# The second mixers' attention loop: steps of four jobs in place of steps of one, and keys stored without zero halves

## The reference

```python
def hybrid_mixer(h, ...):                       # h: 256 x 1024
    (sb_q, sb_k, sb_v, nq, nkc, nvc, nks, nvs, nkw, nvw, ngate,
     dq, dk, dv, iq, ik, iw) = jnp.split(h @ w_in, offs, axis=-1)
    o_a = stick_breaking_attention(...)         # 4 heads
    o_b = nsa_attention(...)                    # 8 heads of 64, 2 groups of keys
    o_c = dsa_attention(...)                    # 4 heads of 64, one shared key head
    g_a, g_b, g_c = jnp.split(jax.nn.sigmoid(h @ w_gate), 3, axis=-1)
    merged = g_a * (o_a @ w_br_a) + g_b * (o_b @ w_br_b) + g_c * (o_c @ w_br_c)
    return merged @ w_out

# nsa_attention, per query block of 128:
#   g0 * (softmax over 15 compressed keys) + g1 * (softmax over selected keys)
#     + g2 * (softmax over the last 512 keys)      with 256 positions all blocks are selected
# dsa_attention, per query block: softmax over the 64 keys that the indexer scores highest
```

## Time and profile before

| | us |
|---|---|
| device time, median of 3 runs | 2225.49 |
| lowest and highest of the 3 | 2224.66, 2225.7 |
| the profiled execution's own time | 2224.94 |
| its span in the profile | 2223.1 |
| TensorE busy in the span | 2214.6 (100%) |
| VectorE busy | 1831.6 (82%) |
| ScalarE busy | 1129.0 (51%) |

### The profile page before, as it was taken

How to read it: one execution, slowest core, us unless ns; L and a number is a source line. 1 busy time by engine, 2 the same in 40 slices (tenths; PEclk the granted TensorE clock), 3 DMA queues, 4 the chain that set the end, 5 groups by cost and what they waited for, 6 DMA issues and landing times.

```text
span 2223.1 us, 42390 instructions
## 1 busy us (share of the span) xinstructions
PE 2214.6 (100%) x16116; PEld 2043.3 (92%) x16116; DVE 1831.6 (82%) x3007; ACT 1129.0 (51%) x1503; POOL 4.8 (0%) x10
## 2 busy tenths in 40 slices
PE   9999999999999999999999999999999999999999
PEld 8998999999998999999999889999999998999998
DVE  8888578888888668887988878888898887898887
ACT  5445565445444565444434676654454346766443
POOL 0000000000000000000000000000000000000000
PEclk9999999999999999999999999999999999999999
DMA  7555445555555445654556443555556545344663
GB/s 253 194 196 202 149 174 196 198 198 170 200 198 203 175 142 188 211 196 163 200 188 211 171 145 130 181 199 190 187 177 207 189 170 191 129 150 165 217 198 132
DMA packets 76816, 407.62 MB, mean 183 GB/s; under 512 B 9264, under 2 KB 9920, under 8 KB 44336
## 3 DMA queue, kind: packets, MB, share of 16 engines
q1 hardware_dynamic: 75792, 404.93, 53.0%
q10 hardware_dynamic: 720, 0.89, 0.1%
q0 software_dynamic: 208, 0.49, 0.1%
HBM read 405.23 MB, written 1.05 MB: 183 GB/s over the span
## 4 chain that ended last, share of the span: by engine, by line
PE 96%; DVE 3%; issue 1%; ACT 0%; DMA 0%; DVEq 0%; SPq 0%
PE ps_proj L684 13%; PE ps_aux L693 13%; PE ps_y L263 10%; PE ps_y L264 10%; PE ps_y L265 10%; PE ps_proj L688 7%; PE ps_aux L696 7%; PE ps_proj L1126 3%; PE ps_proj L1119 3%; PE ps_proj L1120 3%; PE ps_proj L263 2%; PE ps_proj L264 1%; PE ps_proj L265 1%; PE ps_aux L651 1%; PE ps_proj L651 1%; PE ps_aux L1963 1%
## 5 line engine op out<-in xcount | busy, mean ns | idle before, releaser
L130 DVE TENSOR_TENSOR w_lo_front<-w_raw_front,w_hi_front 128x2048 fp32r<-128x2048 f32 x238 | 544.0, 2286 | 36.4 <-ACT w_hi_front L105 36.2
L105 ACT CAST w_hi_front<-w_raw_front 128x2048 fp32r<-128x2048 f32 x238 | 453.0, 1903 | 179.4 <-PE ps_aux L696 144.8
L263 PE MATMUL ps_y<-hidden_lo,w_hi_back 128*128 128x256 f32 x1344 | 372.4, 277 | 0.1
L264 PE MATMUL ps_y<-hidden_hi,w_lo_back 128*128 128x256 f32 x1344 | 371.1, 276 | 0.0
L265 PE MATMUL ps_y<-hidden_hi,w_hi_back 128*128 128x256 f32 x1344 | 371.1, 276 | 0.0
L105 ACT CAST w_hi_back<-w_raw_back 128x1024 fp32r<-128x1024 f32 x248 | 259.9, 1048 | 145.8 <-PE ps_y L265 119.5
L887 ACT ACTIVATE silu_gate<-silu_gate 128x256 f32<-128x256 f32 x176 | 73.7, 418 | 508.7 <-DVE silu_gate L924 508.6
L684 PE MATMUL ps_proj<-xt_lo_hi,w_hi_front 128*128 128x512 f32 x1280 | 319.7, 392 | 0.0
L693 PE MATMUL ps_aux<-xt_lo_hi,w_hi_front 128*128 128x512 f32 x1280 | 319.6, 392 | 0.0
L130 DVE TENSOR_TENSOR w_lo_back<-w_raw_back,w_hi_back 128x1024 fp32r<-128x1024 f32 x248 | 302.3, 1219 | 6.0 <-ACT w_hi_back L105 5.1
L684 PEld LDWEIGHTS ps_proj<-xt_lo_hi,w_hi_front 128*128 128x128 f32 x1280 | 228.5, 188 | 39.5
(11 more groups left out here) (460 smaller groups left out, 3808.0 us busy)
## 6 DMA issues: line engine op xcount, KB each, us to landing
w_raw_front<-in_stream SPq DMA_DIRECT2D x251, 1024.0 KB, 4.9
w_raw_back<-in_stream SPq DMA_DIRECT2D x252, 512.0 KB, 3.5
m_rel_bias<-in_rel_bias SPq DMA_DIRECT2D x2, 2048.0 KB, 7.9
m_params<-in_params SPq DMA_DIRECT2D x2, 656.0 KB, 4.2
w_raw_front<-in_stream SPq DMA_DIRECT2D x4, 256.0 KB, 6.8
w_raw_front<-in_stream SPq DMA_DIRECT2D x2, 512.0 KB, 8.6
x<-in_x ACTq DMA_DIRECT2D x3, 256.0 KB, 6.8
out<-x SPq DMA_DIRECT2D x3, 256.0 KB, 2.3
```

The source lines that it names most:

```text
L105: self.nc.scalar.copy(self.hi[part][:, parity], self.raw[part][:, parity]).then_inc(self.hi_done[part], by)
L130: eng.tensor_tensor(self.lo[part][:, parity], self.raw[part][:, parity], self.hi[part][:, parity].bitcast(F32), ALU.subtract).then_inc(sel ...
L263: nc.tensor.matmul(out, ah, bl, start=start, stop=False)
L264: nc.tensor.matmul(out, al, bh, start=False, stop=False)
```

## The change

Five steps of four jobs (`QUADS`) take the place of twenty steps of one. In a step TensorE does the scores of all four jobs, then the values of the step before, then four gates with the transposes between them: two jobs' behind the first gate, one behind the second and one behind the third. The first job's transposes go to the lower half of `ps_y2` and the second's to the upper half, so that these two don't wait for each other. Score banks, maxima, sums and probabilities have four places in place of two or three. The outputs of a step are 256 columns, rounded in one pair of VectorE instructions in place of two pairs of 128. The weights' remainders and the sorting rounds stand at listed places in the step (`EARLY_LOW`, `MIDDLE_LOWS`, `LATE_LOWS`, `SORTS`). The keys are stored as `m2_kT`, 64 rows for each head of the pair, without the place for the other half (`m2_k_block`), and so without the clearing of it on GpSimd. After the loop the first two channel blocks of the branch products are done for the first six of their eight inputs before the last two of either.

```diff
-DSA_JOBS = [(p, i, 3) for p in range(DSA_HEADS // 2) for i in range(TT)]
+DSA_JOBS = [(p, i, 3) for i in range(TT) for p in range(DSA_HEADS // 2)]
 JOBS = NSA_JOBS + DSA_JOBS
...
+QUADS = len(JOBS) // 4
+LOOP_GATE = GATES - len(JOBS)
+def score_bank(s, job, e):
+    r, width = job % 4, (JOBS[job][1] + 1) * P
+    pair = (s.py[3], s.pa[1]) if r < 2 else (s.py[0], s.py[1])
+    return pair[e][:, r % 2 * width:(r % 2 + 1) * width]
+def quad_out(s, job):
     p, i, br = JOBS[job]
...
+    return s.pa[p if br == 3 else 0][:, i * P:(i + 1) * P]
...
+EARLY_LOW = {2: ((0, 13),)}
+MIDDLE_LOWS = {0: ((1, 10),), 1: ((1, 11), (0, 12)), 2: ((1, 13),), 3: ((1, 14), (0, 15)),
+               4: ((1, 15),)}
+LATE_LOWS = {0: ((0, 11),), 1: ((1, 12),), 2: ((0, 14),), 3: ((0, 16),),
+             4: ((1, 16), (0, 17), (1, 17))}
+SORTS = (3, 4, 5, 4)
...
-    m.pT = s.over_h
+    few = sb("m2_probsT_few", [P, 2, 2, P], F32)
+    m.pT = [few[:, 0], few[:, 1], s.over_h[:, 0], s.over_h[:, 1]]
     m.qT = sb("m2_qT", [P, 6, T], F32)
-    m.kbd = sb("m2_k_block", [P, NKV, 2, T], F32)
+    m.kT = sb("m2_kT", [P, NKV, T], F32)
...
-    m.scs = (sc[:, 0], sc[:, 1], zv[:, 0])
+    m.scs = (sc[:, 0], sc[:, 1], zv[:, 0], zv[:, 1])
...
     def turn(job):
-        i = JOBS[job][1]
+        r, i = job % 4, JOBS[job][1]
         need("probs_ready", job + 1)
-        if job >= 1:
+        if r != 1 and job > 0:
             need("probsT_ready", job)
+        bank = s.py[2][:, (r == 1) * 2 * P:]
         for e in range(2):
             for kc in range(i + 1):
                 j = e * (i + 1) + kc
-                last = nc.tensor.transpose(s.py[2][:, j * P:(j + 1) * P],
-                                           m.scs[job % 3][:, j * P:(j + 1) * P], s.ident[:])
+                last = nc.tensor.transpose(bank[:, j * P:(j + 1) * P],
+                                           m.scs[r][:, j * P:(j + 1) * P], s.ident[:])
         mark.inc(last, "probsT_done")
...
-    def values(job0):
...
+    def values(quad):
+        jobs = range(4 * quad, 4 * quad + 4)
+        if quad == 0:
             need("cs_ready", 1)
             need("pcT_ready", 1)
         else:
-            need("o_ready", pair)
-        for job in (job0, job0 + 1):
+            need("o_ready", quad)
+        need("probsT_ready", 4 * quad + 4)
+        for job in jobs:
             p, i, br = JOBS[job]
-            out = out_bank(s, job0)[:, (job % 2 if br == 3 else 0) * P:][:, 0:P]
             if br == 1:
-                nc.tensor.matmul(out, m.vbd[:, 2 * p:2 * p + 2].rearrange("p h d -> p (h d)"),
-                                 m.pcT[:, i * P:(i + 1) * P], start=True, stop=False)
-            need("probsT_ready", job + 1)
+                nc.tensor.matmul(quad_out(s, job), m.vbd[:, 2 * p:2 * p + 2].rearrange("p h d -> p (h d)"),
+                                 m.pcT[:, i * P:(i + 1) * P], start=i == 0, stop=False)
+        for job in jobs:
+            p, i, br = JOBS[job]
             for e in range(2):
                 for kc in range(i + 1):
                     v = {1: m.zi[:, kc, ZI_NVS + p // 2 * DH:][:, 0:DH],
                          2: m.zn[:, kc, ZN_NVW + p // 2 * DH:][:, 0:DH],
                          3: m.zn[:, kc, ZN_DV:ZN_DV + DH]}[br]
-                    last = nc.tensor.matmul(out[e * DH:(e + 1) * DH], v,
-                                            m.pT[:, job % 2, e * (i + 1) + kc],
-                                            start=br == 3 and kc == 0, stop=kc == i and br != 1)
-            mark.inc(last, "pv_done")
...
+    def scores(quad):
+        if quad >= 1:
+            need("biased", 4 * quad)
+        for job in range(4 * quad, 4 * quad + 4):
+            p, i, br = JOBS[job]
+            kv = {1: p // 2, 2: NSA_GROUPS + p // 2, 3: NKV - 1}[br]
+            qc = p + (NSA_HEADS // 2 if br == 3 else 0)
+            for e in range(2):
+                rows = slice(e * DH, (e + 1) * DH)
+                last = nc.tensor.matmul(score_bank(s, job, e), m.qT[rows, qc, i * P:(i + 1) * P],
+                                        m.kT[rows, kv, 0:(i + 1) * P])
+            mark.inc(last, "scores_done")
+    def branch(c, ks):
         q = P2_Y + c
-        if c < 2:
-            need("gate_ready", GATES - 1 + c)
-        else:
-            need("gated", 2 * (c - 1))
         hi, lo = w.chunk(pe, base, slot0 + q // 3, q % 3)
-        for k in range(8):
+        for k in ks:
             if c == 0 and k >= 2:
-                need("o_ready", {6: 11, 7: 12}.get(k, 2 * (k - 1)))
+                need("o_ready", k - 1)
             out = (s.pj[c % 2][:, 0:T] if k < 2 else s.pj[c % 2][:, T:2 * T] if k < 6
                    else s.pa[c % 2][:, 0:T])
             cols = slice(k * P, (k + 1) * P)
             last = product(nc, out, (hi[:, cols], lo[:, cols]), (m.oh[:, k], m.ol[:, k]),
                            k in (0, 2, 6), k in (1, 5, 7))
-        w.taken(last, q % 3)
+        if ks[-1] == 7:
+            w.taken(last, q % 3)
+    for quad in range(QUADS):
+        scores(quad)
+        if quad >= 1:
+            values(quad - 1)
+        gate(LOOP_GATE + 4 * quad)
+        turn(4 * quad)
+        turn(4 * quad + 1)
+        gate(LOOP_GATE + 4 * quad + 1)
+        turn(4 * quad + 2)
+        gate(LOOP_GATE + 4 * quad + 2)
+        turn(4 * quad + 3)
+        gate(LOOP_GATE + 4 * quad + 3)
+        if quad == 0:
+            turn_compressed()
+    values(QUADS - 1)
+    need("gate_ready", GATES - 1)
+    branch(0, range(6))
+    need("gate_ready", GATES)
+    branch(1, range(6))
+    branch(0, (6, 7))
+    branch(1, (6, 7))
+    for c in range(2, KD):
+        need("gated", 2 * (c - 1))
+        branch(c, range(8))
     project_out(s, s.nh, s.nl, w, base, slot0, P2_O, mark, layer)
...
+            last = nc.scalar.copy(m.kT[rows, j0:j1], s.py[b][rows, at:at + (j1 - j0) * T]
                                   .rearrange("p (a t) -> p a t", a=j1 - j0))
...
     def turned(job):
-        if job >= 2:
-            need("pv_done", job - 1)
-        b, width = job % 2, 2 * (JOBS[job][1] + 1)
-        need("probsT_done", job + 1)
-        mark.inc(nc.scalar.copy(m.pT[:, b, 0:width].rearrange("p j q -> p (j q)"),
-                                s.py[2][:, 0:width * P]), "probsT_ready")
...
+    def exponents(job):
+        r, kw = job % 4, (JOBS[job][1] + 1) * P
+        need("biased", job + 1)
+        for e in range(2):
+            at = m.scs[r][:, e * kw:(e + 1) * kw]
+            mark.inc(nc.scalar.activation(at, at, ACT.Exp, scale=-1.0, bias=m.nmax[:, r, e:e + 1],
+                                          accum_out=m.sum[:, r, e:e + 1]), "exp_ready")
+    for quad in range(QUADS):
+        for job in range(4 * quad, 4 * quad + 4):
+            exponents(job)
+        gate(LOOP_GATE + 4 * quad)
+        turned(4 * quad)
+        turned(4 * quad + 1)
+        gate(LOOP_GATE + 4 * quad + 1)
+        turned(4 * quad + 2)
+        gate(LOOP_GATE + 4 * quad + 2)
+        turned(4 * quad + 3)
+        if quad == 0:
+            chunk(P2_GATE[LOOP_GATE + 3], False)
+            gate_out(LOOP_GATE + 3)
             need("pcT_done", 1)
             mark.inc(nc.scalar.copy(m.pcT[:], s.pa[0][:, 0:T]), "pcT_ready")
-        if TURN_LAG <= step <= LAST_STEP:
-            turned(step - TURN_LAG)
-        if step == LAST_STEP:
-            chunk(P2_GATE[GATE_AT[step - 1]], False)
-            turned(len(JOBS) - 1)
-        if step < len(JOBS):
...
+    def masked_job(job):
+        p, i, br = JOBS[job]
+        r, kw = job % 4, (i + 1) * P
+        need("scores_done", (job | 1) + 1)
+        if job >= 4:
+            need("probsT_done", job - 3)
+        bias = (m.dbias if br == 3 else m.causal)[:, i, 0:kw]
+        head = 2 * p + (NSA_HEADS if br == 3 else 0)
+        for e in range(2):
+            at = slice(e * kw, (e + 1) * kw)
+            last = masked_scores(nc, m.scs[r][:, at], m.nmax[:, r, e:e + 1],
+                                 score_bank(s, job, e), bias, qscale[:, i, head + e:head + e + 1])
+        mark.inc(last, "biased")
...
+    def outs(quad):
+        need("pv_done", quad + 1)
+        for n in range(1 if quad < QUADS - 1 else 2):
+            at, out = (slice(0, P), 2 + quad + n), s.pa[n][:, 0:T]
+            mark.inc(nc.vector.tensor_copy(m.oh[at], out), "o_hi")
+            after("o_hi")
+            mark.inc(nc.vector.tensor_tensor(m.ol[at], out, m.oh[at].bitcast(F32),
+                                             ALU.subtract), "o_ready")
...
+    for quad in range(QUADS):
+        job = 4 * quad
+        if quad == 0:
+            after("acc_ready")
+        if job == len(NSA_JOBS):
+            after("dbias_ready")
+        masked_job(job)
+        masked_job(job + 1)
+        masked_job(job + 2)
+        lows(EARLY_LOW.get(quad, ()))
+        probs(job)
+        probs(job + 1)
+        masked_job(job + 3)
+        lows(MIDDLE_LOWS.get(quad, ()))
+        probs(job + 2)
+        if quad >= 1:
+            outs(quad - 1)
+        probs(job + 3)
```

(70 more changed lines are left out.)

107 lines of the change are left out of this document (15 added, 92 removed).

## The result

The changed kernel takes 2227.78 us (median of 20 runs, 2227.14 to 2228.67), the kernel before 2225.16 (20 runs, 2224.02 to 2226.02). The ratio is 1.0013 with a 95% interval from 1.0007 to 1.0018: 2.6 us longer, inside the 0.2% that were called "same". The profiled execution took 2227.86 with a span of 2226.1, against 2224.94 and 2223.1.

What follows compares the result with a forecast made beforehand. TensorE was taken as the bound (96% of the last chain). Edges saved against new waits gave +1.5 us a layer, +3.0 in two, taken as +2.5: 2228.0 us against a median of 2225.49, range 2222.5 to 2231.5, called "same".

Steps and rivals of the forecast that it cites:

- Edges saved: TensorE's changes between kinds of work in the loop: 5.0 us a layer before, 3.5 after; 1.7 saved was taken.
- The first step: Loop start, VectorE three microseconds late: TensorE waits 1.3, 0.5 and 0.5 us at transposes and bank, 2.3 a layer.
- The remainder's wait: TensorE's 0.7 us loop wait for a front remainder of the weights should go, leaving 1.6 us a layer net loss.
- Third step: Loop jobs 8 to 11: TensorE waits 1.1 us a layer for job 9's copy before job 10's transposes.
- Fourth step: Loop, job 14's transposes: VectorE comes 0.8 us late into the step, so TensorE waits 0.3 us a layer.
- After the loop: Branch products: wait of about 0.5 us ahead of the third channel block, 0.3 gained on outputs' rounding; net 0.2 lost.
- Sum: Whole kernel: -1.7 + 1.6 + 1.1 + 0.3 + 0.2 = +1.5 us a layer, +3.0 for two; +2.5 taken.
- VectorE as the bound: Rival, loop: VectorE cannot work ahead across steps; 1.5 us a layer more, sum +5.5, 2231 us; chance 0.22.
- Shorter waits: Rival, loop: edges save 2.5 us, later waits vanish; -0.7 to -1.9 a layer, down to 2221.5 us; chance 0.12.
- the keys change nothing: Score matmuls: keys without zero halves read the same rows and columns, GpSimd's clearing is off the path; no effect.

Runs made afterwards that it cites:

- the kernel with the values in two halves: Changed kernel with each step's values split, two jobs' ahead of the first gate and two behind it; 2229.22 us, 1.0019 against the kernel before.
- the moved remainder: Changed kernel with front remainder (0, 13) moved from ahead of job 8's scaling to behind job 11's masking; 2227.65 us, 1.0012 against the kernel before.
- the moved sorting round: Changed kernel with one 1.2 us VectorE sorting round moved from the loop's third step to its second; 2226.64 us, 1.0009 against the kernel before.
- whole blocks: Changed kernel with the first two output channel blocks after the loop done in one stretch of eight inputs each; 2226.19 us, 1.0006 against the kernel before.
- the fastest version: Changed kernel with remainder, sorting round, whole-block, two-gates-first and early-copy changes, plus two remainders behind the third job's scaling; 2219.55 us, 0.9977 against the kernel before.
- the two kernels with this wait: Changed kernel with two gates ahead of its first transposes, 2228.30 us; the same plus remainder and sorting moves and whole channel blocks, 2223.14 us.

## Why the prediction was right

**Forecast and size.** 2228.0 was said and 2227.78 measured. The mechanism was as said, changes of kind saved against new waits. That the number is this close is partly luck: 0.5 us a layer more of waits and some 0.6 us that TensorE gave back beyond the 1.7 nearly cancel.

**Edges saved: right, in mechanism and in size.** Worked out: 5.0 us a layer before, 3.5 after, 1.5 saved, of which 1.7 was taken. The loops grew by 1.06 and 1.32 us (84.56 to 85.62, 84.25 to 85.57) while the waits in them grew by 3.40 and 3.60, so TensorE gave back 2.34 and 2.28 beside the waits. Not all of it is edges. An edge shows like this, after the change: the first gate matmul starts 0.20 us behind the last of the values, which are 0.05 to 0.06 apart, and the next is 0.23 behind it instead of 0.12.

```profile
1342.74 0.66 PE L1955 MATMUL ps_aux<-turned_store,m_z_heads 128*64 128x128 f32 x8
1343.33 0.39 PE L1119 MATMUL ps_proj<-xn_lo_hi,w_hi_front 128*128 128x256 f32 x1
1343.56 0.28 PE L1120 MATMUL ps_proj<-xn_lo_hi,w_hi_front 128*128 128x256 f32 x1
1343.67 0.28 PE L1119 MATMUL ps_proj<-xn_lo_hi,w_hi_front 128*128 128x256 f32 x1
```

Summed over the four distances from each change of kind on, less the usual distances, the edges cost 5.4 us a layer before and 3.8 after, in both layers alike: 1.6 saved. The two edges to gates that were priced at 0.10 measure 0.09 (the first score comes 0.206 behind the last gate matmul instead of 0.117) and 0.11 (the 0.23 above). That the changes of kind are what is paid is shown by the kernel with the values in two halves: 1.2 us for four stretches more.

**What the sum lacked.** The other 0.7 to 0.8 us a layer lie elsewhere. Before the change TensorE had short stops that the view of waits does not name, such as this one, for another front remainder: 0.23 between starts where 0.11 is usual, and 0.22 behind it.

```profile
1386.40 0.28 PE L1120 MATMUL ps_proj<-xn_lo_hi,w_hi_front 128*128 128x256 f32 x1
1386.63 1.19 PE L1126 MATMUL ps_proj<-xn_lo_hi,w_lo_front 128*128 128x256 f32 x8
```

With those ahead of transposes at 1375.72 and 1961.15, and with the slower starts behind every wait counted in both kernels, they are worth some 0.4 us in the first layer and 0.2 in the second. In the rest, 0.2 to 0.35 is in gate matmuls that come 0.113 us apart in place of 0.118 more often after the change; why they do stays open.

The page TensorEngine Tiling (Array Packing) of the Trainium skill, Key Properties, has the engine drained at a change of mode, and with the latency of TensorE: Matmul & The Clock Gate (Single matmul latency) that gave an estimate of 2.0 us a layer, 0.163 for each change. The edges by themselves come out lower: 1.6 us for 12 changes fewer is 0.13 each, and 1.2 for the eight more of the values in two halves is 0.15. The rows' 1.5 to 1.7 is the nearer.

**The first step.** Said: 1.3, 0.5 and 0.5, sum 2.3. Measured: 1.31, 0.44 and 0.70, sum 2.45. VectorE's first masking is at 1325.55 against 1325.62 before, and the transposes of job 0 at 1328.30 where "about 1328.3" was worked out. The third is 0.70 and not 0.5. Not foreseen: that these 2.45 are worth only half if TensorE's order alone is mended.

**The remainder's wait** of the earlier trace rows (0.87 and 0.66 counted by starts) went in both layers, as said.

**Third step.** Said 1.1 ahead of job 10; measured 1.29 and 1.30. (The terms given for TensorE add up to S + 9.7 and not 9.8, so the wait to 1.2; and the 18.2 and 17.4 of the next step to 18.0 and 17.3.) The releaser is ScalarE's copy, at the end of the chain that was followed: front remainder, scalings, job 11's exponentials, the cast of a front part, the gate's copy.

**Fourth step.** Said 0.3 ahead of job 14; measured 0.53. The step of the argument, VectorE coming late out of the third step, is what the moved remainder and the moved sorting round show.

**After the loop.** Said 0.2 net, with a wait of 0.5 ahead of the third block; measured 6.29 - 6.10 = 0.19 and 0.66. With whole blocks the stretch is 5.65 in the new order where it was 6.10 in the old. The 0.45 lies in the first block, which took 3.37 us before and 2.93 there, with distances of 0.28, 0.22 and 0.22 at its last two inputs (from 1409.57 on). So what the last outputs cost before (0.3 was the estimate) is gone with or without the split.

**Sum.** Measured by layer: -2.3 + 3.5 + 0.2 = +1.4, against +1.5. The last matmul starts 2.90 us later (2219.47 to 2222.37), the profiled executions differ by 2.92 and the medians by 2.62, so the truth lies between the plain sum of +3.0 and the +2.5 taken. That waits let lateness be made up later is not seen: the first loop ends 1.01 us later than before, the second starts 1.17 later and ends 2.50 later. So the step from +3.0 to +2.5 had no ground that shows; it brought the number nearer by luck. The kernel before had a median 0.3 lower here than in the three runs that the forecast stood on.

**The rivals.** VectorE as the bound did not cost its 1.5 us a layer more, yet it is the right picture of how the later waits hang together, and of the fastest version. "Shorter waits" was wrong on the waits, which were longer than worked out, and its 2.5 for the edges was 1.6, though TensorE gave back 2.3 in all. That the keys change nothing is shown.

## What to carry to other kernels

Batching the steps of a software pipeline saves what the engine pays between kinds of work, here 0.13 to 0.15 us for each change, but takes away the distance at which other engines could work ahead; count both before choosing the size of a step, and mend the order on the helping engines (copies of banks ahead of exponentials, long remainders behind the scaling that is waited for) together with it. When a wait is moved by reordering, find the engine's last pause: only work carried across that pause, or out of the chain, shortens anything, and the rest changes the job at which one waits. Here a gap of two microseconds on TensorE cost in some executions some 1.5 us more in clock, so look at the granted clock behind every new wait.

## What the runs showed of the hardware that was not expected

- Behind a 2.0 us wait of TensorE, with the engine busy before and after, the clock fell to 0.51 in one layer, and behind 1.9 us not in the other. The run times of the two kernels with this wait stand in three groups, 1.3 to 2.5 us apart, which I read as falls in none, one or both layers in different executions. The waits of 1.3 us had no such effect in any profiled execution.
- The same gate matmul of 256 columns at the full clock comes at two paces, 0.118 us apart and 0.113, behind a first distance of 0.20 to 0.23. Of the twenty gates of the first loop after, four keep the first pace throughout, seven the second (2.69 to 2.71 us from first to last start), and nine go over from the first to the second on the way. The kernel before has both as well. What decides it was not tried.
